# A transformer-like stack on one core: norms by one matmul with a block of ones and Ln/Exp on ScalarE, and the rotary swaps of layer 2 moved into the middle of the next tile

## The reference

```python
# layer 1 (first_block)
h = rms_norm(x, norm_mix_pre); proj = h @ w_in
attn = sliding_window_sink_attention(q, k, v, ...); rw = rwkv7_time_mix(p, ...)
x = x + rms_norm(concat(attn, rw) @ w_out, norm_mix_post)
f = conv_gated_ffn(rms_norm(x, norm_ffn_pre), w_ffn_up, conv_w, conv_b, w_ffn_down)   # 1024 -> 2*4096 -> 1024
x = x + rms_norm(f, norm_ffn_post)
# layer 2 (even): h = rms(x); fox attention and differential attention (rotary on q, k; each of its
#   outputs normed per 128 features), @ w_out; then a conv-gated feed-forward of width 2816
# layer 3 (odd): h = rms(x); sparse latent attention with an indexer (top-k) and a normed key-value
#   vector, stick-breaking attention, @ w_out; then the same kind of feed-forward
out = rms(x, final_norm)

def rms_norm(x, g):
    return x * rsqrt(mean(x * x, axis=-1) + 1e-6) * g
```

## Time and profile before

| | |
|---|---|
| median of 3 runs | 2458.31 us (2449.61 to 2460.06) |
| the profiled execution | 2458.13 us |
| its span, first to last instruction | 2456.3 us |
| mean granted clock of TensorE | 0.960 |
| TensorE busy | 2295.8 us, 93% |
| VectorE, ScalarE, GpSimd busy | 1343.2, 865.8, 792.4 us |
| table loads on ScalarE | 24, of 1.28 us each |

### The profile page before, as it was taken

One profiled execution on the slowest core, in us unless ns is written; L12 is line 12 of the kernel. 1 busy time (PEld: TensorE's weight loads), 2 busy tenths in 40 slices (PEclk: granted clock), 3 DMA queues, 4 the chain that ended last, 5 costly groups with the idle time before them and its releaser, 6 DMA issues. The chain is left out here.

```text
span 2456.3 us, 32514 instructions
## 1 busy us (share of the span) xinstructions
PE 2295.8 (93%) x11689; PEld 1855.8 (76%) x11689; DVE 1343.2 (55%) x2258; ACT 865.8 (35%) x1355; POOL 792.4 (32%) x378
## 2 busy tenths in 40 slices
PE   5999998889999999998999999999898799999998
PEld 4777997678878888775776788877676557888876
DVE  4487643487721774154456577721497662677601
ACT  3415111443322333233434333322324563433322
POOL 2000000424443444432213344444464004444442
PEclk8999986889999999999999999999999999999999
DMA  3320000323332233321212233333332003233232
GB/s 118 95 78 1 1 1 6 87 60 94 94 103 86 85 102 102 88 72 43 78 53 69 81 99 97 90 91 94 78 89 57 1 1 95 77 102 93 85 100 81
DMA packets 346541, 179.78 MB, mean 73 GB/s; under 512 B 16840, under 2 KB 343619, under 8 KB 346443
## 3 DMA queue, kind: packets, MB, share of 16 engines
q1 hardware_dynamic: 344842, 177.36, 25.2%
q10 hardware_dynamic: 1056, 1.06, 0.1%
q0 software_dynamic: 544, 0.06, 0.0%
HBM read 176.33 MB, written 2.13 MB: 73 GB/s over the span
## 5 line engine op out<-in xcount | busy, mean ns | idle before, releaser
L298 POOL TENSOR_TENSOR wlo<-raw,whi 128x1024 fp32r<-128x1024 f32 (+3 forms) x327 | 744.2, 2280 | 1585.8 <-ACT whi L294 925.8
L311 PE MATMUL banks<-xhi,whi 128*128 128x512 f32 x1536 | 611.5, 398 | 5.1 <-DVE cb L1038 3.9
L312 PE MATMUL banks<-xlo,whi 128*128 128x512 f32 x1536 | 602.8, 392 | 0.0
L313 PE MATMUL banks<-xhi,wlo 128*128 128x512 f32 x1536 | 602.6, 392 | 0.0
L311 PEld LDWEIGHTS banks<-xhi,whi 128*128 128x128 f32 x1536 | 291.5, 190 | 72.9 <-issue 9.1
L312 PEld LDWEIGHTS banks<-xlo,whi 128*128 128x128 f32 x1536 | 291.2, 190 | 63.4 <-issue 3.8
L313 PEld LDWEIGHTS banks<-xhi,wlo 128*128 128x128 f32 x1536 | 290.9, 189 | 61.1
L879 ACT ACTIVATE whi<-raw 128x1024 fp32r<-128x1024 f32 (+1 forms) x216 | 209.7, 981 | 191.3 <-DMA raw<-in_ffn_w_out_dram 87.7
L967 ACT ACTIVATE cb<-banks,conv 128x512 f32<-128x512 f32 x152 | 117.9, 778 | 445.9 <-DVE banks L1027 445.9
L311 PE MATMUL banks<-ghi,whi 128*128 128x512 f32 x608 | 239.7, 394 | 19.7 <-DVE xT L1069 13.8
L312 PE MATMUL banks<-glo,whi 128*128 128x512 f32 x608 | 238.2, 392 | 0.0
(11 more groups left out here) (453 smaller groups left out, 3081.9 us busy)
## 6 DMA issues: line engine op xcount, KB each, us to landing
raw<-in_ffn_w_in_dram SPq DMA_DIRECT2D x88, 512.0 KB, 3.9
raw<-in_w_ffn_up_dram SPq DMA_DIRECT2D x64, 512.0 KB, 4.1
raw<-in_w_ffn_down_dram SPq DMA_DIRECT2D x32, 512.0 KB, 4.3
raw<-in_ev_w_in_dram SPq DMA_DIRECT2D x25, 512.0 KB, 4.0
raw<-in_ffn_w_out_dram SPq DMA_DIRECT2D x32, 384.0 KB, 3.7
raw<-in_ffn_w_out_dram SPq DMA_DIRECT2D x32, 320.0 KB, 3.3
raw<-in_od_w_in_dram SPq DMA_DIRECT2D x20, 512.0 KB, 3.9
raw<-in_w_in_dram SPq DMA_DIRECT2D x19, 512.0 KB, 3.9
```

The lines of the kernel that those rows point to most:

```text
L298: return pool.tensor_tensor(wlo[c][:, 0:n, :], raw[b][:, 0:n, :], whi[c][:, 0:n, :].bitcast(F32), ALU.subtract)
L311: pe.matmul(acc, whi[b][:, k, :], hi(k), start=first and k == 0, stop=False)
L312: pe.matmul(acc, whi[b][:, k, :], lo(k), start=False, stop=False)
L313: mm = pe.matmul(acc, wlo[b][:, k, :], hi(k), start=False, stop=last and k == n - 1)
```

## The change

1. *Norms of the whole width.* `Rstd` becomes one float32 matmul of a 128x128 block of ones with `acc` (128x512), so that every partition gets the sum of each token. ScalarE then computes Ln(sum/1024 + epsilon), in the bank itself, and Exp(-0.5 x), into `rs` or the bank. VectorE's two steps, the spread and the copy to `rs` are gone, and with them the places of the spread (`SPREAD`).
2. *Norms by token.* `final`, the norm over 128 features and the key-value norm keep their matmuls; Ln and Exp take the place of scaling, Sqrt and reciprocal.
3. *Order on ScalarE in Post.* The first norm is now a call of its own, `act_first`, ahead of the two weight splits that stand at the start of the stage; it begins with a Ln of one column (`warm`). The `norm` helper, which nothing calls, is dropped.
4. *Swaps of layer 2.* The swap of tile m-1 stands behind the first half of tile m and behind `units(m, 0)`, and VectorE's `take(m - 1)` behind its `units(m, 0)` for m above 8.

```diff
     class Rstd:
+        def pe(self, pe, tile):
+            pe.matmul(bank[self.base][:, :], ones, tile, start=True, stop=True).then_inc(self.summed.h, 1)
+
+        def act(self, act, to, done):
+            act.wait_ge(self.summed.h, 1)
+            act.activation(bank[self.base][:, :], bank[self.base][:, :], ACT.Ln, scale=1.0 / D, bias=eps[:, 0:1]).then_inc(self.logged.h, 1)
+            act.wait_ge(self.logged.h, 1)
+            act.activation(to, bank[self.base][:, :], ACT.Exp, scale=-0.5).then_inc(done.h, 1)
...
     class Post:
+        def act_first(self, act):
+            act.activation(self.warm[:, :], eps[:, :], ACT.Ln)
+            self.first.act(act, self.first.of(), self.first.spread)
...
         def act_after(self, act):
-            self.rs.act(act)
+            self.rs.act(act, feed["rs"], self.known)
...
# ffn, ScalarE (even_mixer alike)
+                if lead:
+                    lead.act_first(act)
                 for j in range(AHEAD):
                     hi_in_loop(act, up0 + j + AHEAD, 0, KD)
                 if lead:
                     lead.act(act)
...
# even_mixer, TensorE
                     if m >= lead.TILES:
-                        if m - 1 in ROT[2:] and m > DIFF:
-                            swap(m - 1)
                         pe.wait_ge(w_lo.h, s0 + m + 1)
...
                         dense(m, 0, KD // 2)
                         if m in (4, 5):
                             swap(m - 4)
-                        if m - 1 in ROT[2:] and m <= DIFF:
+                        units(m, 0)
+                        if m - 1 in ROT[2:]:
                             swap(m - 1)
-                        units(m, 0)
...
# even_mixer, VectorE
-                    if m >= 1:
+                    if m >= 1 and not (m > DIFF and m - 1 in ROT):
                         take(m - 1)
...
                     units(m, 0)
+                    if m > DIFF and m - 1 in ROT:
+                        take(m - 1)
                     units(m, 1)
...
# final, ScalarE (TokenRstd): the sums by token stay
+            act.activation(self.st[:, 0, 0:1], eps[:, 0:1], ACT.Ln).then_inc(self.logged.h, 1)
+            act.wait_ge(self.summed.h, 1)
+            act.wait_ge(self.logged.h, 1)
+            act.activation(self.st[:, 0, :], bank[self.base][:, 0:NT], ACT.Ln, scale=1.0 / D, bias=eps[:, 0:1]).then_inc(self.logged.h, 1)
+            act.wait_ge(self.logged.h, 2)
+            act.activation(self.st[:, 1, :], self.st[:, 0, :], ACT.Exp, scale=-0.5).then_inc(self.inverted.h, 1)
```

More of the change, by code:

```diff
@@ L461, in dve @@
[L461 to L510, removed]
@@ new lines, in __init__ @@
+        def __init__(self, base):
+            self.base = base
+            self.summed, self.logged, self.spread = (sig(n) for n in ("sums", "logged", "spread"))
+        def pe(self, pe, tile):
[5 more added lines that the diff above has]
+            act.activation(to, bank[self.base][:, :], ACT.Exp, scale=-0.5).then_inc(done.h, 1)
@@ new lines, in of, with __init__, pe @@
+        def of(self):
+            return bank[self.base][:, :]
+    class TokenRstd:
+        def __init__(self, ctx, base):
+            self.base, self.st = base, sb(ctx, "st", [P, 2, NT])
+            self.summed, self.logged, self.inverted = sig("sums"), sig("logged"), sig("inverted")
+        def pe(self, pe, tile):
+            for t in range(NT):
+                mm = pe.matmul(bank[self.base][:, t:t + 1], tile[:, t * P:(t + 1) * P], ones[:, 0:1], start=True, stop=True)
+            mm.then_inc(self.summed.h, 1)
+        def act(self, act):
+            act.activation(self.st[:, 0, 0:1], eps[:, 0:1], ACT.Ln).then_inc(self.logged.h, 1)
[4 more added lines that the diff above has]
+            act.activation(self.st[:, 1, :], self.st[:, 0, :], ACT.Exp, scale=-0.5).then_inc(self.inverted.h, 1)
@@ L690, in project @@
         tiles_ = lead.TILES if lead else 0
-        lag = lead.SPREAD if lead else 0
+        lag = 4 if lead and tiles_ else 0
         with ExitStack() as ctx:
@@ L730, in _ @@
                         lead.pe_sums(pe)
-                    if lead and m == lead.SPREAD:
-                        lead.pe_spread(pe)
                     if m >= 1:
@@ L2114, in _ @@
                     if m == NORM + 1:
-                        act.wait_ge(meaned.h, 1)
-                        act.activation(st[:, 1, :], st[:, 0, :], ACT.Sqrt).then_inc(rooted.h, 1)
+                        act.wait_ge(totalled.h, 1)
+                        act.activation(st[:, 0, :], bank[7][:, 0:4 * NT], ACT.Ln, scale=1.0 / (2 * HD), bias=eps[:, 0:1]).then_inc(logged.h, 1)
+                        act.wait_ge(logged.h, 1)
+                        act.activation(st[:, 1, :], st[:, 0, :], ACT.Exp, scale=-0.5).then_inc(inverted.h, 1)
                     if m == VB_TURN:
@@ L2317, in act @@
             if m == 14:
+                act.wait_ge(self.summed.h, 1)
+                act.activation(bank[7][:, :], bank[7][:, :], ACT.Ln, scale=1.0 / P, bias=eps[:, 0:1]).then_inc(self.meaned.h, 1)
                 act.wait_ge(self.meaned.h, 1)
-                act.activation(self.sq[:, :], self.part[:, 0, :], ACT.Sqrt).then_inc(self.rooted.h, 1)
+                act.activation(self.sq[:, :], bank[7][:, :], ACT.Exp, scale=-0.5).then_inc(self.rooted.h, 1)
         def dve(self, dve, chain, free):
```

90 lines of the change are left out of this document (24 added, 66 removed).

## The result

The changed kernel takes 2461.53 us (median of 20 runs, 2452.43 to 2471.08), the kernel before 2452.99 us in the same comparison (20 runs). The ratio is 1.0042, with a 95% interval of 1.0025 to 1.0060. It is slower by 0.4%, where 0.6% faster was forecast, and 9.5 us above the upper end of the range. By the medians the change is +8.5 us where -13.6 was forecast: 22 us apart. The profiled execution of the changed kernel has a span of 2468.5 us.

The account below looks back on a forecast made before the run. TensorE, busy 93% of the span, was taken to bound the kernel, by time spent or idled. Terms -14.8 - 3.6 + 1.4 + 2.0 + 0.1 - 0.2 + 1.5 = -13.6 against 2458.13 gave 2444.5 us, range 2437 to 2452.

Parts of the forecast that it names:

- C, the slower one: Layer 2's mixer: TensorE waits for the bank at every one of tiles 10 to 13; 2465.5 us, chance 0.04.
- Swaps, -14.8: Layer 2's mixer: moved swaps end TensorE's 10.1 us wait for ScalarE's copies and keep the clock up, 4.7 us.
- Rival A: Layer 2's swaps: the wait only moves, to the bank or normalised rows; half comes back, 2451.5 us, chance 0.18.
- Sums and spread, -0.9 a stage: Four Ready stages: the new sum matmul costs as much as the old eight, the spread is gained; -3.6 us.
- Post, first norm, +1.4 and +2.0: Layer 1 and mixer: GpSimd's w_lo moves onto the norm's chain and holds VectorE's first rounds; us lost in each.
- Rival D: Post norms: the collisions don't come; Posts win 1.7 and 1.2 us instead of losing 3.4; 2438.2 us, chance 0.12.
- Second norm, +0.1 and -0.2: Post: layer 1 trades spread and copy for Ln, load, Exp (+0.1 us); mixer gains the spread, swap(0) waits (-0.2).
- Final, +1.5: Final norm: Ln, a table load and Exp make the first output copy 1.5 us later.
- Rival B, one set: All norms: one table set serves Ln and Exp, the load between falls away, 5.8 us; 2438.7 us, chance 0.08.

Follow-up runs that it names:

- e1_pad_before: The kernel before plus an unused 32-byte tensor per partition where the changed kernel has eps, nothing else: 2481.28 us, ratio 1.0130 to before.
- e5_norms_only: e2_eps_in_pcol with layer 2's swaps and takes back in their places of before, so the norms' edit alone: 2448.21 us, ratio 0.9978 to before.
- e2_eps_in_pcol: The changed kernel with eps as an extra column of pcol, in former padding; weights, xhi, xlo, ghi at their addresses of before: 2433.51 us, ratio 0.9942 to before.
- e8_one_set: e2_eps_in_pcol with an explicit load, ahead of each norm, of the table set holding both Ln and Exp: 2429.80 us, ratio 0.9896 to before.
- e3_right_down_96: The changed kernel with an unused 96-byte tensor at the right end, so xhi and xlo stand 96 bytes lower: 2451.15 us, ratio 1.0016 to before.
- e7_splits_first: e2_eps_in_pcol with the Post stages' first-norm Ln and Exp behind ScalarE's two weight splits, as the root was before: 2430.39 us, ratio 0.9912 to before.

## Why the prediction was wrong

**The step that failed** is one that isn't in the sum. The prediction went through swaps, sums, spread, loads and the two `Post` norms, and gave the new tensor `eps` no term: it was costed at nothing, and with it the pace of every dense matmul was taken over from before. It costs 31 us (e1_pad_before), and 25 to 28 us in the changed kernel (1.0042 against 0.9942 by the ratios, 2461.53 - 2433.51 by the medians, the two measured beside different runs of before). That is nearly twice what the rest wins, 14 us. None of the rivals had it: C, the slower one, looked for the loss at the swaps. No row of before prices it, but the trace of before shows the two paces: its output projection in layer 2, in which weights and moving operand aren't alike, takes 233 ns a matmul beside 227 elsewhere.

**Swaps, -14.8.** Right in mechanism and near in size: idle gone, clock 1.00, 15.5 to 17.5 us. Rival A is refuted: no bank and no normalised row is late.

**Sums and spread, -0.9 a stage.** From the first dense matmul of layer 2's feed-forward to its first down-projection 242.7 us became 241.1 (e5_norms_only), in layer 3 242.4 became 242.1: 1.6 and 0.3, right on average in the two stages that could be told apart.

**Post, first norm, +1.4 and +2.0.** Right in mechanism and near in size. 10.93 against 9.55 us in layer 1. In the mixer, where TensorE does the changed kernel's sum at a granted clock of 0.50 (it takes 2.04 us), the same span is 11.68 against 9.55, +2.1; in e2_eps_in_pcol, where the clock is 1.00 there and the sum takes 1.10 us, 10.94. TensorE doesn't feel it at once. In e2_eps_in_pcol its first dense matmul comes 8.2 us after the sums instead of 9.0; late are the second norm's sums, 34.5 us after the first ones in both stages, instead of 33.2 and 32.9: +1.4 and +1.6. Rival D, no collisions, is refuted.

**Second norm, +0.1 and -0.2.** Too low in layer 1. From the second norm's sums to the dense matmul that is the 150th behind the first norm, before takes 20.7 us in layer 1 and e2_eps_in_pcol 21.7: +1.0. TensorE's wait for VectorE's cb, which this norm delays, grew from 3.9 to 5.8 us in the groups shown above; the load between Ln and Exp stands at 521.45. In the mixer the two take 15.7 and 15.5, -0.2 as worked out, with a wait of swap(0) of 0.45.

**Final, +1.5.** In the two profiles +1.9 (3.67 against 1.75), but that this is a cost of the change isn't shown. In the kernel with the swaps alone, which has before's own norm, the granted clock over the transposes was 0.61, where it was 1.00 in before:

```profile
2432.05 1.28 ACT L459 ACT_TABLE_LOAD   x1 [0.40 <-PEq L152]
...
2433.78 5.94 PE L2564 MATMUL banks<-cst,xT 128*128 128x128 f32 x32
...
2434.98 0.69 ACT L2573 ACTIVATE res<-banks,st 128x512 f32<-128x512 f32 x1 [0.61 <-PE banks L2564]
```

The first copy is 2.93 us behind the load, the transposes take 5.94 us instead of the 3.69 in before's trace, and the last part of the kernel, from layer 3's first down-projection, is as long with the old norm (142.6 us) as with the new (142.7). At a clock of 0.61 the transposes set the pace: the next three copies of ScalarE wait 0.96, 1.02 and 0.31 us for them. In the profile of after the clock is 0.58 over the transposes, which run from 2458.63 to 2464.87, and Ln, load and Exp (2458.80 to 2460.58) lie beside them. The term was sized by an execution that had a clock of 1.00; that the profiles seem to confirm it is luck. What the new norm costs at a clock of 1.00 no run shows.

**Rival B, one set.** Refuted for the kernel as it is, and its price nearly reached by making it so (4.9 of 5.8). Left to itself, the pair got two loads, in layer 1's Post at 485.05 and 487.11 for the first norm and at 513.59 and 521.45 for the second. With the set natural_log_exp_and_others asked for by name (e8_one_set) it got one, at 475.31 and at 502.68.

**The sum.** With the places kept, -14 us by the ratio (9 to 20) against the -13.6 forecast. That they meet so closely is in part luck: the swaps won up to 3 us more than priced, layer 1's second norm cost 1 us more. What the norms are worth isn't settled. Alone they gain 5 us (0 to 11) where +1.2 was priced; but the kernel with both parts gains 5 us less than the one with the swaps alone, with intervals that overlap. The table's last column gives 6.7 us for the norms without the swaps and 0.9 beside them. About 1 us is in the first half of layer 1's down-projections (96.1 to 96.6 us in the three kernels with the old norm, 94.8 to 95.5 in the others but one, 96.2 in e3_right_down_96), for which I have no mechanism. The rest can't be told from what the clock does.

## What to carry to other kernels

Before pricing a diff's operations, look at what it allocates: compare the SBUF place of each operand of the busiest matmul before and after, and price that like any other edit. Here one float per partition cost more than all the visible edits won. Keep weights and moving operand of dense rounded-float32 matmuls of 512 columns alike mod 256 bytes (226.7 ns here against 233.3), put small tensors where padding is or behind the large ones, and when a stretch that a diff doesn't touch changes its pace, suspect places before engines.

## What the runs showed of the hardware that was not expected

- A 128x512 rounded-float32 matmul behind another takes 226.7 ns from start to start when weights and moving operand are alike mod 256 bytes, 233.3 ns for most other pairs (3%), 228.9 with the weights at 0 and the moving operand 64 or 320 bytes further on. The offsets tried were multiples of 32 bytes. Taking (0, 0) and (32, 32) in turn also gave 233.3. With 256 columns (117.7 ns for the unlike pair, 120.0 for the alike one) and in plain float32 (429.2 ns a row for both) no loss was seen.
- The clock that a stretch gets differs between executions of kernels that do nearly the same work in it. From 300 to 420 us, in the recurrent part of layer 1, the granted clock was 0.79 in before, 0.86 in e2_eps_in_pcol and 0.92 in e7_splits_first, and the stretch from the first to the output projection took 397, 389 and 381 us. The runs of before, 2439 to 2462 us (one of 9147 us left out), spread as widely. A gain of 0.5% has to be read from many runs, or from the trace with this stretch left out.
- Two operations of VectorE on SBUF operands that meet GpSimd's w_lo took 1.71 and 2.85 us instead of 0.75 and 0.69, at the same length in both Posts of the changed kernel.
